# A two-block network on one core: unsplit weights for three projections, the choice of keys spread over the state groups, and small constants computed later

## The reference, cut to what matters

```python
u, q, k, v, qi, ki, wi, g_ssm, g_attn = split(xn @ w_in)
y_ssm = s5_branch(u, ...)          # complex linear scan over the tokens, 32 groups of 64 states
    # ends: y = gelu(y); y = y * sigmoid(y @ w_glu)
y_attn = dsa_branch(q, k, v, qi, ki, wi)
    # score = sum_h relu(qi_h . ki) * wi_h, causal; the 64 best keys of each query are kept;
    # softmax attention over them, 8 heads
merged = sigmoid(g_ssm) * (y_ssm @ w_ssm_up) + sigmoid(g_attn) * (y_attn @ w_attn_up)
h = h + merged @ w_out
# then norm, and 16384 experts with a top-16 choice (peer_ffn), norm
```

## Time and profile before

| | |
|---|---|
| median of 3 runs | 1815.27 us (1812.45 to 1815.41) |
| the profiled execution, its own time | 1806.43 us |
| its span, first to last instruction | 1804.2 us |
| PE busy | 1691.6 us (94%) |
| DVE busy | 1167.7 us (65%) |
| ACT busy | 836.1 us (46%) |
| POOL busy | 730.6 us (40%) |
| mean granted clock of PE | 0.974 of full speed |

### The profile page before, as it was taken

How to read it: one execution, slowest core, us unless ns; L and a number is a source line. 1 busy time by engine, 2 the same in 40 slices (tenths; PEclk the granted TensorE clock), 3 DMA queues, 4 the chain that set the end, 5 groups by cost and what they waited for, 6 DMA issues and landing times.

```text
span 1804.2 us, 26998 instructions
## 1 busy us (share of the span) xinstructions
PE 1691.6 (94%) x10600; PEld 1463.4 (81%) x10600; DVE 1167.7 (65%) x2411; ACT 836.1 (46%) x1453; POOL 730.6 (40%) x394
## 2 busy tenths in 40 slices
PE   6988999989989998998698999999999999999997
PEld 5766999867779987543478999999999988888885
DVE  7463674746457666569543599989999744444444
ACT  5544666344466643012434454534444444545553
POOL 2323568043246740244255699900000044444442
PEclk9998999999999999999799999999999999999999
DMA  7332454553245554333235455444444556666664
GB/s 279 100 104 102 157 198 165 187 187 105 94 151 177 187 190 149 111 115 104 71 117 198 140 177 187 165 148 144 141 141 141 165 182 193 195 192 195 195 189 139
DMA packets 77454, 283.18 MB, mean 157 GB/s; under 512 B 8721, under 2 KB 8977, under 8 KB 77073
## 3 DMA queue, kind: packets, MB, share of 16 engines
q1 hardware_dynamic: 76032, 276.50, 46.8%
q10 hardware_dynamic: 1296, 4.97, 0.7%
HBM read 279.33 MB, written 2.10 MB: 156 GB/s over the span
## 4 chain that ended last, share of the span: by engine, by line
PE 76%; DVE 16%; issue 3%; ACT 3%; POOL 2%; DMA 1%; POOLq 0%; DVEq 0%; ACTq 0%
PE bank L529 62%; PE bank L520 6%; PE bank L584 4%; DVE H L1362 2%; POOL wl L2028 1%; DVE H L1908 1%; DVE H L1902 1%; DVE H L1904 1%; DVE H L1900 1%; DVE H L1906 1%; DVE tab L1373 1%; PE bank L652 1%; ACT wh L1024 1%; PE bank L608 1%; DVE wl L1356 1%
## 5 line engine op out<-in xcount | busy, mean ns | idle before, releaser
L2028 POOL TENSOR_TENSOR wl<-raw,wh 128x1024 fp32r<-128x1024 f32 x223 | 569.3, 2562 | 722.8 <-ACT wh L1024 711.4
L1024 ACT ACTIVATE wh<-raw 128x1024 fp32r<-128x1024 f32 x486 | 503.2, 1050 | 81.4 <-PE bank L529 64.7
L529 PE MATMUL bank<-hh,wh 128*128 128x256 f32 x1872 | 535.3, 286 | 3.6 <-DVE hl L1362 2.0
L529 PE MATMUL bank<-hl,wh 128*128 128x256 f32 x1872 | 527.9, 282 | 0.0
L529 PE MATMUL bank<-hh,wl 128*128 128x256 f32 x1872 | 526.6, 281 | 0.0
L1356 DVE TENSOR_TENSOR wl<-raw,wh 128x1024 fp32r<-128x1024 f32 x263 | 351.4, 1342 | 109.3 <-ACT wh L1024 109.0
L529 PEld LDWEIGHTS bank<-hh,wh 128*128 128x128 f32 x1872 | 356.9, 191 | 5.1 <-POOL wl L2028 4.1
L529 PEld LDWEIGHTS bank<-hl,wh 128*128 128x128 f32 x1872 | 357.0, 191 | 0.0
L529 PEld LDWEIGHTS bank<-hh,wl 128*128 128x128 f32 x1872 | 356.4, 190 | 0.0
L1362 DVE TENSOR_TENSOR acl<-H,ach 128x256 fp32r<-128x256 f32 x128 | 87.6, 685 | 181.5 <-ACT ach L1027 181.5
L529 PE MATMUL bank<-wh,ach 128*128 128x512 f32 x512 | 199.3, 389 | 1.9 <-DVE acl L1362 1.9
(11 more groups left out here) (209 smaller groups left out, 2290.4 us busy)
## 6 DMA issues: line engine op xcount, KB each, us to landing
raw<-in_ut_dram SPq DMA_DIRECT2D x128, 512.0 KB, 3.5
raw<-in_vt_dram SPq DMA_DIRECT2D x128, 512.0 KB, 4.1
raw<-in_wup_dram SPq DMA_DIRECT2D x88, 512.0 KB, 4.1
raw<-in_win_dram SPq DMA_DIRECT2D x48, 512.0 KB, 4.5
raw<-in_wdown_dram SPq DMA_DIRECT2D x44, 512.0 KB, 4.2
raw<-in_wout_dram SPq DMA_DIRECT2D x24, 512.0 KB, 3.6
raw<-in_wga_dram SPq DMA_DIRECT2D x16, 512.0 KB, 3.6
raw<-in_wpq_dram SPq DMA_DIRECT2D x16, 512.0 KB, 3.7
```

The costliest lines, as they stand in the source:

```text
L529: m = p.e.matmul(out, lhs[i][a], rhs[i][b], start=start and i == 0 and j == 0, stop=stop and i == n - 1 and j == 2)
L1024: a.e.activation(high_of(u), raw_of(u), ACTF.Copy).then_inc(act_hi.up(("hi", u)), 1)
L2028: g.e.tensor_tensor(low_of(u), raw_of(u), high_of(u).bitcast(F32), ALU.subtract).then_inc(pool_lo.up(("lo", u)), 1)
```

## The change

- `wglu`, `wsu`, `wau` are no longer split: no `wh`, no `wl`, float32 matmuls from the slot on `gy`, `gt2` (the gated branch) and the whole turned `ya`. The halves of `gy` and `gt2` on ACT and DVE go too.
- `FILL` is now 3, 3, 3, 3, 3, 2, 2, 2 units a round, with `state_in(m+1)` and then `state_out(m)` after them, two more units after the last round, and the last two units of `wga` (`wga3`, in banks 5 and 6) inside the attention stage at c = 0 and 2; their sigmoid is done later, from SBUF, at c = 4. The three turning steps of queries and the four index steps move to earlier places.
- `CHOICE` now runs behind groups 8 to 15: 2, 4, 3, 3, 3, 3, 3, 3 pieces. `product(n+1)` stands behind `scanned(n)` for every group.
- `glu` at c = 4, `wsu` at c = 6, 8, 12, 14. Tile 0 of the attention output is turned at c = 14 and multiplied by `wau` at c = 16 and 18, between the last maps; tile 1 follows. Gating goes tile by tile, and `me` of tile 1 is turned between the tiles of `wout2`'s first slab.
- `opening` runs at k = 0, 8, 10, 12, 13 (ACT's exponents at 9 and 11), `state_constants` at k = 9, 10, 11 and then once for each `f` of layer 0's up projection from f = 2. ACT's sines and cosine move to the start of the up projection.
- Buffers: `hw` and the new `sel_s` lie over `hh` and `hl`; `wh4`, `wl4` have places of their own; slots count from 0. `rel`, `sc`, `mask2` of the choice move into `sel_s`.

The core of the diff:

```diff
-        stage("wglu", [(wglu_d[n], 1024, True) for n in range(2)])
-        stage("wsu", quarters(wsu_d[0]) + quarters(wsu_d[1]))
-        stage("wau", quarters(wau_d[0]) + quarters(wau_d[1]))
+        stage("wglu", [(wglu_d[n], 1024, False) for n in range(2)])
+        stage("wsu", quarters(wsu_d[0], False) + quarters(wsu_d[1], False))
+        stage("wau", quarters(wau_d[0], False) + quarters(wau_d[1], False))
+        OPENING, L_EXPS = (0, 8, 10, 12, 13), (9, 11)
+        STATES = (9, 10, 11)
-        FILL = [(2, 2), (2, 2), (2, 2), (1, 2), (1, 2), (1, 1), (1, 1), (1, 0)]
-        Q_TURNS = {(3, 1): (8, 6), (4, 0): (0, 2), (4, 1): (4, )}
-        CHOICE = {5: 6, 6: 8, 7: 8}
-        IDX = {(4, 1): 0, (5, 0): 2, (5, 1): 4, (6, 0): 6}
-        C_GLU, C_WSU = (4, 5), (9, 11, 13, 15)
+        FILL = [3, 3, 3, 3, 3, 2, 2, 2]
+        Q_TURNS = {(3, 0): (8, 6), (3, 1): (0, 2), (4, 0): (4, )}
+        IDX = {(4, 0): 0, (4, 1): 2, (5, 0): 4, (5, 1): 6}
+        CHOICE = {8: 2, 9: 4, 10: 3, 11: 3, 12: 3, 13: 3, 14: 3, 15: 3}
+        C_GATES, C_GLU, C_WSU, C_WAU = (0, 2), 4, (6, 8, 12, 14), 16
...
             state_in(0)
             for m in range(8):
-                if m:
-                    state_out(m - 1)
-                for half in range(2):
-                    if half and m + 1 < 8:
-                        state_in(m + 1)
-                    for j in Q_TURNS.get((m, half), ()):
+                for f in range(FILL[m]):
+                    next(fill)
+                    for j in Q_TURNS.get((m, f), ()):
                         queries_turned(j)
...
+                if m < 7:
+                    state_in(m + 1)
+                    state_out(m)
+            next(fill)
+            next(fill)
             state_out(7)
...
+                if c == C_WAU - 2:
+                    run(up)
+                    ya_turned(0)
+                if c >= C_WAU:
+                    attention_up(0, (c - C_WAU) // 2)
+            ya_turned(1)
+            attention_up(1, 0)
+            attention_up(1, 1)
+            me_turned(0)
+            run(by_tokens("wout2", first["wout2"], 2, 512, 4, 2, 0, ready_tokens("me"), lambda n, t: (dve_out, ("xa", 2, t, n)), skew=(0, 1),
+                          between=lambda: me_turned(1)))
...
-                    if L or 5 <= k <= 7 or k >= 9:
+                    if L == 0 and k in STATES:
                         next(constants_, None)
...
+                    if L == 0 and f >= 2:
+                        next(constants_, None)
...
+            product(0)
+            for n in range(16):
+                products_summed(n)
+                scanned(n)
+                if n < 15:
+                    product(n + 1)
...
+                for _ in range(CHOICE.get(n, 0)):
                     next(choice)
```

More of the change, by code:

```diff
@@ L204, in program @@
         n_units = len(plan)
[L205 to L206 removed]
+        slot = [i % 6 if i < n_early else (i - n_early) % 4 for i in range(n_units)]
         held, halves_of, before, halved = [], [], {}, {}
@@ L276, in used_by @@
         def used_by(i):
-            whole = first["wu"] <= i < first["wglu"] or first["keys"] <= i < n_early
+            whole = first["wu"] <= i < first["wout2"] or first["keys"] <= i < n_early
             return pe_out if plan[i][2] or whole else dve_out
@@ L908, in glu, with attention_up @@
                 emptied[b] = (dve_out, ("glu", n))
-            up = by_tokens("wsu", first["wsu"], 2, 512, 2, 2, 4, lambda t, k: p.wait_ge(dve_out, ("ysl", k // 2)), lambda n, t: (dve_out, ("gs", n, t)), of=(6, 7))
+            up = by_tokens("wsu", first["wsu"], 2, 512, 2, 2, 0, lambda t, k: p.wait_ge(dve_out, ("glu", k // 2)), lambda n, t: (dve_out, ("gs", n, t)), of=(6, 7), whole=gt2)
+            def attention_up(t, n):
+                b = 2 * t + n
+                for h in range(2):
+                    i = first["wau"] + 2 * n + h
+                    if t == 0:
+                        unit(i)
+                    if h == 0:
+                        claim(b)
+                    p.wait_ge(act_out, ("hT", "ya", t))
+                    for k in range(2):
+                        m = p.e.matmul(banks[b][:, :], hTw[:, 2 * h + k, tcols(t)], unit_whole(i, k, 2, slice(0, 512)), start=h + k == 0, stop=h + k == 2)
+                    if h == 1:
+                        bank_of["wau", n, t] = b
+                        emptied[b] = (dve_out, ("ga", n, t))
+                        m.then_inc(pe_out.up(("mm", "wau", n, t), ("used", i) if t else None), 1)
+                    elif t:
+                        m.then_inc(pe_out.up(("used", i)), 1)
@@ new lines, in act @@
+            for c in range(0, 20, 2):
+                if c == C_GLU:
+                    for _ in fill:
+                        pass
+                for i in pair_of(maps2, c):
+                    exps("d", maps2, att2, i)
+                weights_copied("d", maps2, att2, c - 2)
+                if c == C_GLU:
+                    for t in range(2):
+                        a.wait_ge(act_out, ("ev", "wga", 3, t))
+                        do(gates[:, t, 1536:2048], gates[:, t, 1536:2048], ACTF.Sigmoid, ("gate", t))
@@ L1279, in act @@
-            turned("ya", (0, 1), 1)
-            for i in range(4):
+                        do(banks[7 - n][:, :], banks[7 - n][:, :], ACTF.Sigmoid, ("glu", n))
+                if c >= 10:
+                    stream(first["wsu"] + (c - 10) // 2)
+                if c == C_WAU - 2:
+                    ya_turned(0)
+            ya_turned(1)
+            turned("me", (0, ), 2)
+            for i in range(1, 4):
+                if i == 3:
+                    turned("me", (1, ), 2)
                 stream(first["wau"] + i)
-            turned("me", (0, 1), 2)
```

214 lines of the change are left out of this document (94 added, 120 removed).

## The result

| | before | after |
|---|---|---|
| median of 4 runs of each, side by side | 1814.12 us (1812.45 to 1815.41) | 1795.98 us (1794.14 to 1797.98) |
| the profiled execution: its own time, its span | 1806.43, 1804.2 us | 1794.14, 1792.2 us |
| PE busy | 1691.6 us (94%) | 1697.9 us (95%) |
| mean granted clock, second block's state stage | 0.93 | 0.95 |

The ratio is 0.9905, 95% interval 0.9893 to 0.9916: 18.1 us, 1%, faster. The profiled execution before was itself 6 us under the fastest of the four. The two profiled executions differ by 12.0 us of span only, because the stages that the change leaves alone happened to take longer in the second (layer 0 from its up projection on, layer 1 and the u projection by 1 us each, the experts by 2.2 and 1.9 in two stretches). So I read distances inside a profile, from one event to the next, and not positions.

The account below looks back on a forecast made before the run. It took layer 0's late qkT copies behind small DVE operations, and DVE's key choice beside POOL's low parts, as the bounds. Terms 11.2 + 11.8 + 1.0 - 4.6 = 19.4 us gave 1795.8 us, range 1783 to 1809.

Parts of the forecast that it names:

- Layer 0, 11.2: Layer 0 before its up projection: moving small operations later on DVE gains 11.2 us (2 to 13.5).
- The term for the first wait: Layer 0, PE's idle ahead of the first scores: 2.0 instead of 6.41 us, gaining 4.4, and 0.3 in the scores.
- The term of 6.5 us: Layer 0 from the ninth w_in unit on: 6.5 of the 8.0 us difference to layer 1 goes (bounds 2 and 8.0).
- Constants in the up projection, 0: Layer 0's up projection: 37 moved operations, 28 us, hidden by 44 us of DVE's idle time; costed at nothing.
- The rival called slower: Up projection: 37 constants operations at 2.0 to 2.5 us each exceed DVE's idle time; 1837 us, chance 0.08.
- State stage, 11.8: Second block's state stage: first mask near 855.0 against 866.83, gain 11.8 us; bounds from 28 to the gain gone.
- The queue walk: State stage, group by group: PE waits 1.4, 1.5 and 4.7 us for POOL's products 9, 11, 13, none for 15.
- Attention stage, 1.0: From first mask to wout2: 61.5 us against 62.5, a gain of 1.0 us (-4 to 5).
- `wout2`, loss of 4.6: wout2: three PE waits, 2.5 us, and a turning, 2.2, make it 27.1 instead of 22.5; loss 4.6 (1 to 8).
- Half of it: Rival: the spread choice stalls the groups or layer 0's copies still wait, losing one gain of 11; about 1806 us, chance 0.17.
- more: Rival: PE's stalls shrink and a steadier PE stays at full clock; gain 29.5 us, 1786 us, chance 0.12.
- no change: Rival: layer 0's wait moves to the next copy and the choice loses what it won; near 1814 us, chance 0.05.

Follow-up runs that it names:

- the run with lumps: Changed kernel with the choice in three blocks behind groups 11, 13 and 15, plus eight unused POOL subtractions behind POOL's product of group 15: 1806.5 us.
- that with the choice spread: Changed kernel, choice still behind groups 8 to 15, plus eight unused POOL subtractions behind POOL's product of group 15: 1795.0 us.
- both with POOL busy: Changed kernel plus eight unused POOL subtractions behind the product of group 15, with the choice in three blocks (1806.5 us) or spread (1795.0 us).
- the one with lumps: Changed kernel with the choice in three blocks of 6, 8 and 8 pieces behind groups 11, 13 and 15, no POOL load added: 1796.3 us.
- the split earlier: Changed kernel with ACT splitting one w_out unit ahead of its copies of the merged output's tile 0 instead of behind them: 1794.7 us.
- queries turned later: Changed kernel with the queries turned one unit later in round 3, nothing else: 1785.2 us.
- both repairs: Changed kernel with queries turned one unit later and ACT's split of one w_out unit ahead of its copies: 1788.1 us.
- all four: Changed kernel with queries turned one unit later, choice from group 9, a unit moved from round 7 to 5, ACT's w_out split earlier: 1788.4 us.
- no units behind the rounds: Changed kernel with the two units behind round 7 moved into rounds 4 and 5: 1799.7 us.
- the added load: Eight unused POOL subtractions over 128x1024 put behind POOL's product of group 15 in the changed kernel: 1806.5 us with choice in three blocks, 1795.0 us spread.

## Why the prediction was right, point by point

Predicted were 1795.8 us and 19.4 us of gain; measured 1796.0 and 18.1. That the time was hit to 0.2 us is luck: layer 0 gave 2.4 us less than its term, the attention stage and `wout2` 1.5 more than theirs, and the kernel before ran 1.2 us below the median that the forecast started from. That each stage's gain came near its term is not.

- **Layer 0, 11.2.** 8.8 by the profile, 9.0 by undoing it. The term for the first wait was right (4.4 and 0.3; measured 4.2 and 0.3). The term of 6.5 us for the steps from the ninth unit on measured 4.3: mis-sized. It took nearly all of the difference to layer 1 for the constants, but the first unit stayed at the lower clock, and at 68.26 a wait of 1.74 us for the copy of `qkT` remained, where layer 1 has 1.08. So two of its signs were missed by a little: an idle time of 2.24 us (2 or less was forecast) and a stretch of 103.2 us (101).
- **Constants in the up projection, 0.** Right: 126.0 us to the first matmul of the down projection (127.3 before), PE without a gap. DVE's busy time rose by 9 us, not the 28 of the estimate. The rival called slower needed 1.8 us an operation; a hundred more of them cost 0.59 each. Its mechanism is real, but its price was three times too high; the 35 idle us that were left are worth some 60 such operations (35 / 0.59).
- **State stage, 11.8.** The first mask was forecast 127.6 us after the first unit and came after 127.7. The queue walk held: the turning's wait 5.2 against 4.34, those for products 9, 11 and 13 1.4, 1.5 and 4.7 against 1.02, 2.64 and 3.50, none for 15. The allowance of 3.5 us for units at a lower clock was 4.1 (113.7 us of busy time to the end of `state_out(7)`, against the 109.6 of the sum). The reason given was only half of it. I put the gain down to the spread choice; that POOL would have no low part between 730 and 880 I named only as something to be seen. The runs show that either is enough, and that undoing both brings back 8.5 of the 11.8 us.
- **The rule of the Trainium skill** ("SBUF — State Buffer", section "Who interferes with whom"). The trace agrees for sums with two SBUF operands: 2.5 us beside POOL operations of 2.45 to 2.49, in the earlier trace rows, in the run with lumps and in that with the choice spread. Read strictly it spoke against sums between POOL's products, and there it cost little: a pair that takes 0.76 us took 1.68 where the two met.
- **Attention stage, 1.0.** 2.0 measured; the one wait of 1.8 us that I found is the row at 867.14, 1.85.
- **`wout2`, loss of 4.6.** 4.1 measured, with waits of 1.12 and 0.97 for units and the turning in the middle, as described.
- **Half of it, more, no change** would each have needed one of the two gains of about 10 us to fail or to double. Neither did; they hold apart from each other, as undoing the first left the second as it was (126.9 us to the first mask). What "more" described, shorter stalls and a steadier clock, one moved turning brought later: 1785.2 us, where "more" had 1786.

Open: the 3.3 us of the new order apart from choice and POOL, and why the same wait of 1.85 us is followed by a unit of 5.37 us in some kernels (among them the changed one, both with POOL busy, the one with lumps, the split earlier) and of 3.67 in others (queries turned later, both repairs, all four, no units behind the rounds); no run here varied it alone.

## What to carry to other kernels

When a change cures one wait in two ways at once, its profile can't tell them apart: take back each alone and both together, and put the load that was removed back as a dummy on the other engine. A wait of PE costs more than its length if units behind it run at the lower clock (here 3.5 us less of idle time brought the first mask 5.6 us forward), so after a reordering look first for waits that one unit of other work, moved ahead, would fill. And count the cover of an engine by its idle time in that stage: beyond it each microsecond cost 1.6 here.

## What was not expected of the hardware

- Beside POOL operations of 2.45 us in SBUF, DVE's max and replace (0.43, 0.41) and the sum with one operand in a bank (0.48) kept their times, while a sum with two SBUF operands took 2.5. Of max and replace the prediction had said so. But a tensor-scalar operation with one SBUF operand over 128x256, 0.29 us alone, took 0.90 beside the added load and 1.18 beside the low parts of the kernel before, and nine of 128x16 in the up projection took 0.61 us on average, against 0.17 in the `w_in` steps before.
- The hundred added products of 128x32 with both operands in SBUF took 0.59 us on average, with POOL busy for 0.40 of the stage; the constants' own of 128x16, which stand right ahead of them, took 0.23 in both kernels. The convolution just before releases POOL's own products, so the place in the step may matter as much as the size; that was not varied.
- An idle time of 2.24 us ahead of the first scores was followed by a unit of 4.54 us, almost the same as 6.41 us of idle time (4.63), and 1.85 us by one of 5.37 instead of 3.67. Yet behind 2.64 us, at 813.55, the matmuls took 0.40 us each, and 0.63 behind 3.50, at 827.10. The length of the last wait alone doesn't tell which level follows.
